# Expert weights in units of four k-tiles by 1024 columns, and a long expert that turns its activations in two halves

## What is computed

```python
def run_block(args):
    tok, e = args
    hmid = xt[tok] @ w_gu[e] + b_gu[e]                      # 1024 -> 2048
    glu = jnp.minimum(hmid[:, 0::2], SWIGLU_LIMIT)
    lin = jnp.clip(hmid[:, 1::2], -SWIGLU_LIMIT, SWIGLU_LIMIT)
    act = glu * jax.nn.sigmoid(SWIGLU_ALPHA * glu) * (lin + 1.0)
    return act @ w_down[e] + b_down[e]                      # 1024 -> 1024
y_slots = lax.map(run_block, (slot_tok.reshape(n_blocks, MOE_BLOCK), block_expert)).reshape(-1, D)
```

## Time and profile before

| | us |
|---|---|
| median of 3 runs | 3410.58 |
| lowest, highest | 3408.15, 3414.55 |
| the profiled execution | 3408.74 |
| its span, first to last instruction | 3406.7 |
| PE busy in it | 2880.0 (85%) |
| DVE, ACT busy | 1704.5 (50%), 1078.7 (32%) |

### The profile page before, as it was taken

How to read it: one execution, slowest core, us unless ns; L and a number is a source line. 1 busy time by engine, 2 the same in 40 slices (tenths; PEclk the granted TensorE clock), 3 DMA queues, 4 the chain that set the end, 5 groups by cost and what they waited for, 6 DMA issues and landing times. The chain is left out here.

```text
span 3406.7 us, 36827 instructions
## 1 busy us (share of the span) xinstructions
PE 2880.0 (85%) x13443; PEld 2068.8 (61%) x13487; DVE 1704.5 (50%) x2698; ACT 1078.7 (32%) x1592; POOL 154.2 (5%) x173
## 2 busy tenths in 40 slices
PE   6887879999997799999944358999999999999983
PEld 5656657888776588887732247455556655457541
DVE  3864464444544644444266743744446644257413
ACT  4344333222323432222152123222334433035311
POOL 0530000000000000000012002000000000000001
PEclk9997889999998899999957658999999999999996
DMA  3110213444222122222200004899999899999994
GB/s 119 55 45 25 87 70 134 173 172 163 101 77 91 42 99 99 99 87 85 89 2 0 1 5 167 327 387 388 384 342 337 299 386 356 386 362 327 389 370 175
DMA packets 289694, 622.02 MB, mean 183 GB/s; under 512 B 9603, under 2 KB 15394, under 8 KB 289090
## 3 DMA queue, kind: packets, MB, share of 16 engines
q1 hardware_dynamic: 274816, 568.96, 46.1%
q10 hardware_dynamic: 12322, 41.38, 3.1%
q0 software_dynamic: 2304, 8.39, 0.7%
HBM read 577.54 MB, written 41.16 MB: 182 GB/s over the span
## 5 line engine op out<-in xcount | busy, mean ns | idle before, releaser
L88 DVE TENSOR_TENSOR unit_low<-unit_whole,unit_high 128x4096 fp32r<-128x4096 f32 (+3 forms) x65 | 283.8, 4366 | 191.0 <-ACT unit_high L85 190.7
L85 ACT ACTIVATE unit_high<-unit_whole 128x4096 fp32r<-128x4096 f32 (+3 forms) x65 | 225.6, 3471 | 480.4 <-PE psum L631 309.8
L2896 PE MATMUL psum<-ring_slot,hT 128*64 128x512 f32 x1008 | 306.8, 609 | 10.8 <-DMA ring_slot<-in_moe_w_gu 10.8
L631 PE MATMUL psum<-high_parts,unit_high 128*128 128x512 f32 x640 | 254.2, 397 | 9.0 <-DVE low_parts L88 9.0
L631 PE MATMUL psum<-low_parts,unit_high 128*128 128x512 f32 x640 | 252.0, 394 | 0.0
L631 PE MATMUL psum<-high_parts,unit_low 128*128 128x512 f32 x640 | 251.7, 393 | 0.0
L85 ACT ACTIVATE moe_w_high<-ring_slot 128x1024 fp32r<-128x1024 f32 x208 | 205.8, 1046 | 3.8 <-PE psum L3050 2.2
L631 PE MATMUL psum<-unit_high,hidden_high 128*128 128x512 f32 x512 | 199.6, 390 | 0.0
L631 PE MATMUL psum<-unit_high,hidden_low 128*128 128x512 f32 x512 | 199.3, 389 | 0.0
L631 PE MATMUL psum<-unit_low,hidden_high 128*128 128x512 f32 x512 | 199.2, 389 | 0.0
L631 PE MATMUL psum<-unit_high,high_parts 128*128 128x512 f32 (+2 forms) x448 | 178.4, 398 | 20.9 <-DVE low_parts L88 17.0
(11 more groups left out here) (626 smaller groups left out, 5837.3 us busy)
## 6 DMA issues: line engine op xcount, KB each, us to landing
ring_slot<-in_moe_w_gu SPq DMA_DIRECT2D x102, 2048.0 KB, 18.0
unit_whole<-in_moe_w_gu SPq DMA_DIRECT2D x34, 2048.0 KB, 13.9
ring_slot<-in_moe_w_down SPq DMA_DIRECT2D x34, 2048.0 KB, 13.0
ring_last_slot<-in_moe_w_down SPq DMA_DIRECT2D x34, 2048.0 KB, 17.5
unit_whole<-in_w_up SPq DMA_DIRECT2D x16, 2048.0 KB, 7.6
unit_whole<-in_w_down SPq DMA_DIRECT2D x16, 2048.0 KB, 7.7
expert_rows<-zero_row ACTq DMA_DIRECT2D x15, 1536.0 KB, 5.3
unit_whole<-in_w_in SPq DMA_DIRECT2D x5, 2048.0 KB, 7.7
```

Source lines behind the costliest of these rows:

```text
L85: return act.activation(self.high, self.whole, ACT.Copy)
L88: return dve.tensor_tensor(self.low, self.whole, self.high.bitcast(F32), ALU.subtract)
L631: ins = pe.matmul(bank, a, c, start=(i == 0 and m == 0), stop=(i == len(products) - 1 and m == len(parts) - 1))
L2896: ins = pe.matmul(banks[g], xg[:, c, 0:HALF], w[g][:, c, :], start=(c == 0), stop=False)
```

## The change

A unit of weights becomes four k-tiles by 1024 columns: units 0 and 1 are the upper and lower rows of the first 1024 columns of `w_gu`, 2 and 3 of the second, 4 and 5 the two halves of the rows of `w_down`. A quarter is one k-tile by 1024 columns, and the products of a unit go to two PSUM banks at once. Unit 4 now needs only the first 512 activations of a long expert. They are made, in operations twice as wide, while PE multiplies unit 2, and turned between units 2 and 3. The second half is made while PE multiplies unit 4 and turned between units 4 and 5. Both parts of the gather stand behind that second turn. The three branches of an expert on PE become one, so the gather is in the code twice. A slot is now free when PE's last product of its unit is done (`quarter_used`), not when a PSUM bank is full.

```diff
-QUARTERS = 4
+HALF_K = 4
...
     def up_half(self, pe, j, wait_unit, xg, par, parted=False):
...
-                    ins = pe.matmul(banks[g], xg[:, c, 0:HALF], w[g][:, c, :], start=(c == 0), stop=False)
-            if parted and pair == 1:
-                ins.then_inc(self.quarter_used.sem, PARTED)
+                    ins = pe.matmul(banks[g], xg[:, c, 0:HALF], w[c // HALF_K][:, c % HALF_K, g * 512:(g + 1) * 512],
+                                    start=(c == 0), stop=False)
+            if parted:
+                ins.then_inc(self.quarter_used.sem, 2 * HALF_K if pair else HALF_K + 1)
...
+    def unit_used(self, eng, j, n, parted=False):
+        if parted:
+            eng.wait_ge(self.quarter_used.sem, self.used_at(j, n, HALF_K - 1))
+        elif n < 4:
             eng.wait_ge(self.up_full, 4 * j + n + 1)
         else:
             eng.wait_ge(self.down_full, 2 * j + n - 3)
...
-    def quarter_products(self, pe, j, n, q, bank, a, first, a_low_at=None):
-        w = self.quarter(n, q)
-        pe.wait_ge(self.k.unit_split.sem, self.split_at(j, n, q))
-        for i, (stationary, moving) in enumerate(((a.high, w.high), (a.high, w.low), (a.low, w.high))):
-            if i == 2 and a_low_at is not None:
+    def unit_products(self, pe, j, n, banks, a, first, a_low_at=None):
+        for q in range(HALF_K):
+            w, f = self.quarter(n, q), HALF_K * (n % 2) + q
+            pe.wait_ge(self.k.unit_split.sem, self.split_at(j, n, q))
+            for g in range(2):
+                cols = slice(g * 512, (g + 1) * 512)
+                pe.matmul(banks[g], a.high[:, f, :], w.high[:, cols], start=(first and q == 0), stop=False)
+                pe.matmul(banks[g], a.high[:, f, :], w.low[:, cols], start=False, stop=False)
+            if q == 0 and a_low_at is not None:
                 pe.wait_ge(self.k.unit_split.sem, a_low_at)
-            for c in range(2):
-                ins = pe.matmul(bank, stationary[:, 2 * q + c, :], moving[:, c, :], start=(first and i == 0 and c == 0),
-                                stop=False)
+            for g in range(2):
+                ins = pe.matmul(banks[g], a.low[:, f, :], w.high[:, g * 512:(g + 1) * 512], start=False, stop=False)
+            ins.then_inc(self.quarter_used.sem, 1)
+
+    def turn_act_pair(self, pe, j, pair):
+        k, T = self.k, self.tables
+        pe.wait_ge(self.act_ready, 4 * j + 2 * pair + 2)
+        for i in range(HALF_K):
+            f = HALF_K * pair + i
+            ins = pe.transpose(k.psum[:, 2 + pair, i * P:(i + 1) * P], T.act[:, f * P:(f + 1) * P], k.ident[:, :])
+        ins.then_inc(self.act_turned, 1)
+
+    def expert_parted(self, pe, j, wait_unit, xg, par, gathers):
...
+        early, late, out = ([k.psum[:, b + g, :] for g in range(2)] for b in (2, 4, 6))
+        w = wait_unit(pe, 0)
+        for g in range(2):
+            for c in range(HALF_K):
+                ins = pe.matmul(early[g], xg[:, c, :], w[:, c, g * 512:(g + 1) * 512], start=(c == 0), stop=False)
         ins.then_inc(self.quarter_used.sem, 1)
+        self.unit_products(pe, j, 1, early, T.xg_parts, False)
+        biases(early, T.bias_parts, 0, self.up_full)
+        self.unit_products(pe, j, 2, late, T.xg_parts, True)
+        self.turn_act_pair(pe, j, 0)
+        self.unit_products(pe, j, 3, late, T.xg_parts, False)
+        biases(late, T.bias_parts, 2, self.up_full)
+        pe.wait_ge(self.actT_ready, 2 * j + 1)
+        pe.wait_ge(self.o_whole, 2 * j)
+        self.unit_products(pe, j, 4, out, T.act_parts, True, self.act_low_at(j, 0))
+        self.turn_act_pair(pe, j, 1)
+        for b in gathers:
+            gathers[b](b)
+        pe.wait_ge(self.actT_ready, 2 * j + 2)
+        self.unit_products(pe, j, 5, out, T.act_parts, False, self.act_low_at(j, 1))
+        biases(out, T.down_parts, 0, self.down_full)
+
+    def activate_parted(self, dve, j, xg):
...
+        def clip(pair):
...
+            both = k.psum[:, 2 + 2 * pair:4 + 2 * pair, :].rearrange("p b (f two) -> p b f two", two=2)
+            dve.tensor_scalar(T.glu[:, :, :], both[:, :, :, 0], 7.0, None, ALU.min).then_inc(self.glu_ready, 2)
+            dve.tensor_scalar(T.lin[:, :, :], both[:, :, :, 1], 7.0, -7.0, ALU.min, ALU.max).then_inc(self.lin_ready, 2)
...
+        self.split_xg(dve, j, xg)
+        for q in range(HALF_K):
+            self.split_quarter(dve, j, 1, q)
+        for pair in range(2):
+            n = 2 + 2 * pair
+            for q in range(HALF_K - 1):
+                self.split_quarter(dve, j, n, q)
+            clip(pair)
+            self.split_quarter(dve, j, n, HALF_K - 1)
+            multiply(pair)
+            for q in range(HALF_K):
+                self.split_quarter(dve, j, n + 1, q)
+            split_act(pair)
...
     def act_parted(self, act, j, xg, gatherings, loaded):
         k, T = self.k, self.tables
         self.round_xg(act, j, xg, gatherings)
...
+        self.round_quarters(act, j, 1, loaded)
+        for pair in range(2):
+            self.round_quarters(act, j, 2 + 2 * pair, loaded)
+            act.wait_ge(self.glu_ready, 4 * j + 2 * pair + 2)
+            act.activation(T.sig[:, :, :], T.glu[:, :, :], ACT.Sigmoid, scale=1.702).then_inc(self.gate_ready, 2)
+            self.round_quarters(act, j, 3 + 2 * pair, loaded)
+            act.wait_ge(self.act_turned, 2 * j + pair + 1)
+            act.activation(self.act_tiles(T.act_parts.high, pair), k.psum[:, 2 + pair, :], ACT.Copy)\
+               .then_inc(self.actT_ready, 1)
...
 def expert_unit(k, e, n):
 
+    rows = slice(n % 2 * HALF_K * P, (n % 2 + 1) * HALF_K * P)
     if n < 4:
-        w = k.ins["moe_w_gu_2"][0][bass.ds(e, 1), :, n * 512:(n + 1) * 512]
+        w = k.ins["moe_w_gu_2"][0][bass.ds(e, 1), rows, n // 2 * 1024:(n // 2 + 1) * 1024]
     else:
-        w = k.ins["moe_w_down_2"][0][bass.ds(e, 1), :, (n - 4) * 512:(n - 3) * 512]
+        w = k.ins["moe_w_down_2"][0][bass.ds(e, 1), rows, :]
...
                 with pe.If(half):
                     E.wait_for_up(pe, j, 2 * pair + 2)
                     E.up_half(pe, j, wait_unit_of(i, b), xg, h, parted)
+                    if gathers:
+                        gathers[0](0)
+                    E.turn_act_half(pe, j)
+                    if gathers:
+                        gathers[1](1)
+                    E.down_half(pe, j, wait_unit_of(i, b), h, parted)
                 with pe.Else():
                     E.wait_for_up(pe, j, 2 * pair + 2)
-                    (E.up_parted if parted else E.up)(pe, j, wait_unit_of(i, b), xg, h)
-                if ahead:
-                    E.gather(pe, pair + 1, j + 2, h, 0, saved=2 * (j + 1) + 1)
-                with pe.If(half):
-                    E.turn_act_half(pe, j)
-                with pe.Else():
-                    E.turn_act(pe, j)
-                if ahead:
-                    E.gather(pe, pair + 1, j + 2, h, 1, saved=2 * (j + 1) + 2)
...
                     if parted:
+                        E.expert_parted(pe, j, wait_unit_of(i, b), xg, h, gathers)
```

More of the change, by code:

```diff
@@ L2979, in turn_act @@
                                k.ident[:, :])
[L2980 removed]
+        ins.then_inc(self.act_turned, 2)
     def down(self, pe, j, wait_unit, par):
@@ L3361, in step @@
                 xg = T.xg[:, b // 2, :, h * P:(h + 1) * P]
-                ahead = not (last and b >= 2)
                 parted = not (first and b == 0)
+                gathers = {}
+                if not (last and b >= 2):
+                    for bank in range(2):
+                        gathers[bank] = lambda bank: E.gather(pe, pair + 1, j + 2, h, bank, saved=2 * (j + 1) + bank + 1)
                 with pe.If(half):
```

216 lines of the change are left out of this document (90 added, 126 removed).

## The result

The changed kernel takes 3432.2 us (median of four runs, 3427.7 to 3435.5), the kernel before 3411.0 beside it: a ratio of 1.0061, interval 1.0043 to 1.0078. It is **slower by 21 us** (0.6%), where 3376 was predicted. The profiled execution has a span of 3428.6 us, 21.9 more than before.

A forecast was written before the change was run, and what follows sets the result against it. It took PE (busy 1065 of 1138.7 us in the expert stage) and DMA (98%) as both near full. Terms −37.3 + 5 − 2 = −34.3 us took 3408.74 to 3374.4, so 3376 us as median, range 3362 to 3400.

The forecast's parts named there:

- Part 4: PE's three branches per expert become one: next product starts perhaps 0.1 us sooner, 2 us won, bounds 0 to 4.
- rival C: PE's instructions come late at jumps over a long expert's code: 62 us, 3438, up to 3490 with clock; chance 0.08.
- Part 1: Turn in two halves in long experts: PE's waits there and slow clock go, 37.3 us won, upper bound 42.
- Rivals A and B: A: transfers take back more of the gain, 3390, chance 0.16. B: DVE late in long experts, 3393, chance 0.15.
- Part 2: Weight slots and transfers: time saved in long experts comes back as short experts' waits for DMA, 5 us given back.
- Part 3: Weight loads with 4 KB instead of 2 KB rows: 0 to 4% less DMA work, 0 to 5 us, taken as 0.

The follow-up runs named there:

- shared gathers: The changed kernel with PE's step in three branches again, both gathers shared by long and short experts, in place of one branch: 3346.9 us, ratio 0.9816.

## Why the prediction was wrong

- **What failed is Part 4**, "three branches become one", costed at 2 us won, and with it the 0.08 given to rival C. The merged branch costs 86.5 us of the stage, more than everything else wins. The rival's mechanism was right in kind and its price low: it had 3.45 us at each of 18 short experts, 62 us, and more with the clock. What the row that I leant on shows (84 products, nothing) was true and stayed true there; the step from 84 to 174 had no row. A cost with no row should have been bounded by the nearest one, the loop's start with 3.45 us, so 0 and 62 us are both ends of its range. I took the first as the forecast and left the second out of the range.
- The rival's 3438 us lies 6 us from the 3432.2 measured, and that is luck: it priced the jumps at 62 us, where 86.5 were lost, and took 34.3 for the gain of the rest, where it is 64.6.
- What the rival missed: a jump can cost more than one such wait. From short to long two jumps follow each other, and 7.6 to 8.0 us are paid; the start of a round went from 3.45 to 10.8. The time lost is 91.8 − 11.1 us of waits and 17 of PE's busy time.
- **Part 1 was right**, and a little low. With the layout mended the thirteen long experts take 543.8 us for 586.3, 42.5 won (43.8 with the wait at the one round start in neither sum); predicted 37.3, upper bound 42. One takes 40.9 us and not 41.6. The terms of the 41.6 that were too high: unit 0 takes 6.45 us and not 6.9, since the 6.89 of the earlier trace rows hold a bias that the sum counts once more; the two turns take 0.35 us each and not 1.05 together. DVE's new operations take 0.68 to 0.69 us each, as the earlier trace rows had it. The last long expert waits 2.4 us in place of 3.1 and takes 40.2 for 40.8. Rivals A and B did not come: besides the waits of that last expert, PE waits for DVE's splits 2.7 us in two places, and less for weights than before (below).
- **Part 2** (5 us given back to the transfers): with shared gathers PE waits 11.0 us for weights, for 13.5 before, so nothing was given back. In the kernel with 2 KB rows in two loads it is 26.0, 12.5 more, of which the second load may be 3.6 (14.6 against 11.0, both with 4 KB rows): such waits do come, and with rows of 4 KB they did not.
- **Part 3** (rows of 4 KB, 0, bounds 0 to 5): mis-sized. Saturated engines move 5% more; the medians of the kernels with 2 KB and 4 KB rows differ by 26 us, 9 of the 30 between their traces inside the stage. The earlier trace rows had the 4% in them. The eighteen short steps take 507.6 us with shared gathers for 525.8.
- Without the merged branch the parts come to −60.7 us in the stage and −64.6 in the median, where I had −34.3: below the range on the other side.

By the Trainium skill ("Runtime: NRT & Kernel Launch", instruction fetch mechanics), instructions come in blocks of 256, and a taken branch out of the two blocks held must fetch first. A product is two instructions in the page of the profile (13443 on PE and 13487 on PEld), so, as an estimate by that page, 128 products make a block. The trace agrees on the block: TensorE's instruction packets are of 16 KB (151 packets, 2.47 MB before), where the section says 16 KiB. By blocks of 128 products, as the same estimate, a jump of up to 128 ends in the block where it starts or in the next, and a longer one goes further or not by where it starts; that more places wait from 116 over 140 to 174, and always the same ones, agrees with it. The 3.6 to 3.8 us at jumps over 90 do not, and no run here moved a jump of over 128 without changing its length. The same section gives PE a store of 2048 instructions. By that a jump over 174 products would have stayed inside, and no run here agrees with it.

## What to carry to other kernels

Count the code between two instructions that run one after the other, the parts for other cases included. Here jumps over up to 116 products were free at nearly all places (two over 90 were not); beyond 130 a jump cost 1 to 3.5 us at some places in the code and nothing at others, up to 8 us where two came together, and a lower clock afterwards between two experts; cut a long branch by shared work in between, or write the loop out. A wait that no engine explains ("issue"), right behind a branch, is the sign. When a change bundles a new order with a new code layout, cost the layout as a part of its own, with the worst row of the trace as one end of the range.

## What the runs showed of the hardware

- Instructions that never run slow a kernel down: 96 transposes per step, 33 us.
- The wait at a round start from short to long grew from 3.3 to 9.5 us when the loop became 96 transposes longer, and was 5.1 with 384 more in the kernel before (8.8 with 192). With 9.5 us three packets of instructions came in place of one. The start from long to short stayed at 1.0 to 1.3 us in the kernels with shared gathers (4.35 before). I have no rule for that.
- The same number of products jumped over (90) cost nothing in one kernel and 3.6 to 3.8 us at two of three places in another. With 140 products only the short experts that stand second in a round waited, all four of them. Whether a jump waits goes with its place in the code as well as with the distance; what about the place decides it was not tried.
- A wait of 10.8 us was followed by 9.60 us for unit 0 at a granted clock of 0.76, one of 3.45 us by 9.87 us at 0.72: the longer one brought no more slow time.
- Weight loads of 4 KB rows ran at 408 GB/s where those of 2 KB rows ran at 387. By the Trainium skill ("DMA: Bandwidth & Descriptors", SWDGE vs HWDGE vs iDMA) a packet is preferably of up to 4096 bytes; the section says it of transfers that GpSimd issues. The loads here are issued by SyncE, and for them the runs show 5% more rate with packets of that size than with twice as many of half.
